# Ten of the 31 taps of three depthwise convolutions moved from VectorE to TensorE, in a two-layer hybrid decoder trunk

## What is computed

```python
a, gate = _split(h, (CONV_WIDTH, CONV_WIDTH))          # 512 channels each
z = a * jax.nn.sigmoid(gate)
z = jnp.pad(z, ((0, 0), (CONV_KERNEL - 1, 0), (0, 0)))   # CONV_KERNEL = 31
y = lax.conv_general_dilated(z, conv_w[:, None, :], ..., feature_group_count=CONV_WIDTH)
y = y + conv_b
return jax.nn.silu(_layernorm(y, ln_g, ln_b, LN_EPS))
```

## Time and profile before

| | us |
|---|---|
| median of 3 runs | 1245.67 (1244.42 to 1250.74) |
| profiled execution, its own time | 1247.64 |
| its span, first to last instruction | 1245.8 |
| PE busy in the span | 1208.2 (97%) |
| VectorE / ScalarE / GpSimd busy | 635.9 / 405.9 / 497.3 |
| mean granted TensorE clock | 0.986 |

### The profile page before, as it was taken

One profiled execution on the slowest core, in us unless ns is written; L12 is line 12 of the kernel. 1 busy time (PEld: TensorE's weight loads), 2 busy tenths in 40 slices (PEclk: granted clock), 3 DMA queues, 4 the chain that ended last, 5 costly groups with the idle time before them and its releaser, 6 DMA issues. The chain is left out here.

```text
span 1245.8 us, 19823 instructions
## 1 busy us (share of the span) xinstructions
PE 1208.2 (97%) x7876; PEld 965.5 (78%) x7876; DVE 635.9 (51%) x1032; ACT 405.9 (33%) x582; POOL 497.3 (40%) x368
## 2 busy tenths in 40 slices
PE   7999999999999999999999999989999999999996
PEld 5877778888888888886777767657888888888885
DVE  5524655442114544455988878976545210444333
ACT  5634423222112222227444535443322211222110
POOL 0541435554445555544121201113545444555441
PEclk9999999999999999999999989979999999999998
DMA  7212222232232223322111001102223222223211
GB/s 278 102 68 68 80 90 71 98 101 102 101 101 81 90 99 102 101 102 69 35 69 35 36 35 36 36 2 95 75 101 101 102 101 100 72 97 101 102 67 68
DMA packets 17776, 104.97 MB, mean 84 GB/s; under 512 B 1968, under 2 KB 2480, under 8 KB 6064
## 3 DMA queue, kind: packets, MB, share of 16 engines
q1 hardware_dynamic: 17280, 103.67, 24.0%
q10 hardware_dynamic: 432, 0.38, 0.1%
HBM read 101.94 MB, written 2.10 MB: 84 GB/s over the span
## 5 line engine op out<-in xcount | busy, mean ns | idle before, releaser
L582 POOL TENSOR_TENSOR w_lo<-w_raw,w_hi 128x512 fp32r<-128x512 f32 x360 | 491.6, 1396 | 715.4 <-ACT w_hi L675 266.5
L1015 PE MATMUL ps<-h_hi,w_hi 128*128 128x512 f32 x688 | 275.9, 401 | 0.1
L1015 PE MATMUL ps<-h_lo,w_hi 128*128 128x512 f32 x688 | 268.4, 390 | 0.0
L1015 PE MATMUL ps<-h_hi,w_lo 128*128 128x512 f32 x688 | 268.4, 390 | 0.0
L675 ACT ACTIVATE w_hi<-w_raw 128x2048 fp32r<-128x2048 f32 x50 | 95.6, 1912 | 194.7 <-PE ps L1015 143.4
L1015 PEld LDWEIGHTS ps<-h_hi,w_hi 128*128 128x128 f32 x688 | 129.3, 188 | 37.4 <-issue 10.9
L1015 PEld LDWEIGHTS ps<-h_hi,w_lo 128*128 128x128 f32 x688 | 129.3, 188 | 27.6
L1015 PE MATMUL ps<-f_hi,w_hi 128*128 128x512 f32 x384 | 149.4, 389 | 0.0
L1015 PE MATMUL ps<-f_lo,w_hi 128*128 128x512 f32 x384 | 149.4, 389 | 0.0
L1015 PE MATMUL ps<-f_hi,w_lo 128*128 128x512 f32 x384 | 149.4, 389 | 0.0
L1015 PEld LDWEIGHTS ps<-h_lo,w_hi 128*128 128x128 f32 x688 | 129.5, 188 | 25.7 <-issue 1.0
(11 more groups left out here) (328 smaller groups left out, 1705.1 us busy)
## 6 DMA issues: line engine op xcount, KB each, us to landing
w_raw<-in_weights SPq DMA_DIRECT2D x91, 1024.0 KB, 4.9
x<-in_xT SPq DMA_DIRECT2D x8, 256.0 KB, 6.3
w_raw<-in_weights SPq DMA_DIRECT2D x8, 256.0 KB, 6.9
outT<-x SPq DMA_DIRECT2D x8, 256.0 KB, 2.0
sgu_ln<-in_sgu_ln SPq DMA_DIRECT2D x1, 512.0 KB, 7.2
low_w<-in_low_w SPq DMA_DIRECT2D x1, 512.0 KB, 5.7
...
```

Of the source, the lines that this page charges most:

```text
L582: piece = pool.tensor_tensor(w_lo[:, j, at], w_raw[:, j, at], w_hi[:, j, at].bitcast(f32), SUB)
L1015: mm = pe.matmul(bank(gb(g) if isinstance(i, int) else g % 2), w, r, start=(k == 0 and m == 0), stop=(k == K - 1 and m == 2))
```

## The change

TensorE takes the last ten taps (j = 21 to 30) of groups 1, 2 and 3. ScalarE makes, for each of these 30 taps, a diagonal matrix: the 128x128 identity times the tap's weight of each partition (`diag`, into one of the two halves of a new buffer `tapd`). PE multiplies this diagonal by the shifted window of `zpad` (`ptap`, a float32 matmul of 128x128 by 128x512) and sums five taps in one PSUM tile, so there are two such tiles in each group. They have tile numbers of their own at the end of chunks 6, 8 and 10 of the projection, and so they use banks 0 and 1 in turn with the projection's tiles. VectorE adds each of the six sums to `cv` by one instruction (`padd`): those of groups 1 and 2 before tap 0, those of group 3 after taps 9 and 19. Group 0 keeps its 31 taps on VectorE. Several one-off semaphores are merged into one, `set_up`, with rising counts; the mask buffer is smaller by 896 bytes per partition. All three lists are written anew.

```diff
-MIX1 = [2] * 11
+MIX1 = [2, 2, 2, 2, 2, 2, 4, 2, 4, 2, 4]
+PE_CHUNK = {1: 6, 2: 8, 3: 10}
+PE_TAPS = 5
+PE_AFTER = {1: (0, 0), 2: (0, 0), 3: (10, 20)}
+N_V = [31, 21, 21, 21]
...
-        masks = sb("masks", [P, 4104], u8)
+        masks = sb("masks", [P, 3208], u8)
...
+            tapd = sb("tapd", [P, 2, P])
...
+        def pe_tile(c, q):
+
+            return FIRST_TILE[N_MIX1 + PE_CHUNK[c]] + 2 + q
+
+        def pe_tap(c, j):
+
+            return 2 * PE_TAPS * (c - 1) + j - N_V[c]
...
         PE1 = [
...
+            ("slice", 8, 4), ("slice", 8, 5), ("tok_tr", 1, 0), ("slice", 8, 6), ("slice", 8, 7),
+            *run("slice", 10, 0, 7), ("scores", 1, 1), ("slice", 10, 7), ("tok_tr", 1, 1), ("tok_tr", 1, 2),
+            ("scores", 1, 2), *run("ptap", 1, 21, 28), ("scores", 1, 3), ("ptap", 1, 28), ("ptap", 1, 29),
+            ("zw", 2), ("ptap", 1, 30), ("za", 2), ("tx", 1, 3, 0), ("tx", 1, 3, 1), ("post", 0, 0),
+            ("dx", 1, 3, 0), ("dx", 1, 3, 1), *run("slice", 9, 0, 8), ("tx", 1, 4, 0), ("tx", 1, 4, 1), ("ks", 2),
...
+            ("slice", 11, 0), ("dx", 1, 6, 0), ("dx", 1, 6, 1), *run("slice", 11, 1, 8), ("ptap", 2, 21),
+            ("g", 1, 0), ("ptap", 2, 22), ("ptap", 2, 23), ("u", 1, 0), ("s", 1, 0), ("ptap", 2, 24),
+            ("ptap", 2, 25), ("post", 0, 2), ("bonus", 2), ("g", 1, 1), ("corner", 2), ("ptap", 2, 26), ("y", 1, 0),
+            ("u", 1, 1), ("slice", 13, 0), ("slice", 13, 1), ("s", 1, 1), ("y", 1, 1), ("ptap", 2, 27),
+            ("ptap", 2, 28), ("g", 1, 2), ("ptap", 2, 29), ("ptap", 2, 30), ("u", 1, 2), ("s", 1, 2), ("y", 1, 2),
...
+            *run("slice", 21, 4, 8), ("tok_tr", 3, 0), ("scores", 3, 1), *run("ptap", 3, 21, 24), ("scores", 3, 2),
+            ("tok_tr", 3, 1), *run("ptap", 3, 24, 27), ("tok_tr", 3, 2), ("post", 2, 0), ("scores", 3, 3),
+            ("ptap", 3, 27), ("ptap", 3, 28), ("tx", 3, 3, 0), ("tx", 3, 3, 1), ("dx", 3, 3, 0), ("dx", 3, 3, 1),
+            ("tx", 3, 4, 0), ("tx", 3, 4, 1), ("post", 2, 1), ("dx", 3, 4, 0), ("dx", 3, 4, 1), ("ptap", 3, 29),
+            ("ptap", 3, 30), ("tx", 3, 5, 0), ("tx", 3, 5, 1), ("conv_mean", 0), ("dx", 3, 5, 0), ("dxt", 3, 5),
...
         ACT1 = [
...
+            ("evac_q", 8), ("diag", 1, 21), ("tok_tr", 1, 0), *run("diag", 1, 22, 29), ("cut", 54, 0),
+            ("cut", 54, 1), ("diag", 1, 29), ("cut", 54, 2), ("tok_tr", 1, 1), ("diag", 1, 30), ("zw", 2),
...
+            ("g", 3, 0), ("u", 3, 0), ("g", 3, 1), ("u", 3, 1), ("conv_sq", 0), ("conv_sq", 1),
+            ("cut", 58, 3), ("g", 3, 2), ("u", 3, 2), ("conv_sq", 2), ("conv_sq", 3), ("m", 1), ("m", 2),
...
+            def diag_(c, j):
+                i = pe_tap(c, j)
+                if i >= 2:
+                    group, n = divmod(i - 2, PE_TAPS)
+                    if n == PE_TAPS - 1:
+                        act.wait_ge(s("gemm_done"), pe_tile(1 + group // 2, group % 2) + 1)
+                    else:
+                        act.wait_ge(s("ptap_mm"), (PE_TAPS - 1) * group + n + 1)
+                act.activation(tapd[:, i % 2, :], IDENT, ACT.Copy, scale=col("conv_w", TAPS * c + j)).then_inc(s("tapd_done"), 1)
...
+            def ptap(c, j):
+                i = pe_tap(c, j)
+                q, n = divmod(j - N_V[c], PE_TAPS)
+                g = pe_tile(c, q)
+                pe.wait_ge(s("tapd_done"), i + 1)
+                if n == 0:
+                    pe.wait_ge(*freed(g))
+                    pe.wait_ge(*evacuated(g1(15 + 2 * c)))
+                    pe.wait_ge(*set_up("zpad"))
+                mm = pe.matmul(bank(g % 2), tapd[:, i % 2, :], zpad[:, c % 2, j:j + SEQ], start=(n == 0), stop=(n == PE_TAPS - 1))
+                mm.then_inc(s("gemm_done" if n == PE_TAPS - 1 else "ptap_mm"), 1)
...
             def tap(c, j):
...
-                if j == 0:
+                if j == 0 and not (c and PE_AFTER[c][0] == 0):
                     ts(cv[:, c, :], zpad[:, c % 2, 0:SEQ], col("conv_w", TAPS * c), col("conv_b", c), MUL, ADD)\
...
+            def padd(c, q):
+                g = pe_tile(c, q)
+                dve.wait_ge(s("gemm_done"), g + 1)
+                if PE_AFTER[c][q] == 0 and q == 0:
+                    ts(cv[:, c, :], bank(g % 2), col("conv_b", c), 0.0, ADD, ADD).then_inc(s(f"gemm_evac{g % 2}"), 1)
+                else:
+                    dve.wait_ge(*in_cv(c, PE_AFTER[c][q], q))
+                    tt(cv[:, c, :], cv[:, c, :], bank(g % 2), ADD).then_inc(s(f"gemm_evac{g % 2}"), 1)
```

More of the change, by code:

```diff
@@ L385, in build @@
         PE1 = [
[L386 to L405, removed]
@@ L488, in build @@
-            ("s", 3, 1), *run("tap", 3, 25, 31), ("s", 3, 2), ("m", 2), *run("conv_sub", 0, 4), ("conv_root",),
-            ("conv_scale", 0), ("conv_scale", 1), ("post_v", 3, 0), ("conv_scale", 2), ("conv_scale", 3),
-            ("post_v", 3, 1), ("m", 3), ("post_v", 3, 2), ("m", 4), ("post_v", 3, 3), *run("m", 5, 8),
+            ("zero", 0), ("zero", 1), ("stat",), *run("zero", 2, 6), ("evac_a", 0), ("evac_b", 0), ("evac_a", 2),
+            ("evac_b", 2), ("evac_a", 4), ("zero", 6), ("evac_b", 4), ("evac_a", 3), ("scan", 0), ("evac_b", 3),
@@ new lines, in build @@
+            ("dyn", 2, "rk"), ("evac_a", 11), ("s", 1, 0), ("bonus", 2), ("tap", 1, 16), ("post_v", 0, 3),
+            ("padd", 2, 0), ("evac_b", 11), ("corner", 2), ("s", 1, 1), ("solve", 2, 6), ("solve", 2, 5),
+            ("solve", 2, 4), ("solve", 2, 3), ("solve", 2, 2), ("padd", 2, 1), ("s", 1, 2), *run("tap", 2, 0, 6),
+            ("scores", 2, 0), *run("tap", 2, 6, 9), ("scores", 2, 1), ("scores", 2, 2), ("tap", 1, 17),
+            ("scores", 2, 3), ("solve", 2, 1), ("x_of", 2), ("scan", 3), ("tap", 2, 9), ("tap", 2, 10),
@@ new lines, in build @@
+            ("u", 1, 0), ("diag", 2, 24), ("diag", 2, 25), ("cut", 55, 3), ("diag", 2, 26), ("evac_q", 11),
+            ("diag", 2, 27), ("scores", 2, 0), ("g", 1, 1), ("u", 1, 1), *run("diag", 2, 28, 31), ("cut", 56, 0),
+            ("g", 1, 2), ("u", 1, 2), ("g", 1, 3), ("u", 1, 3), ("tok_tr", 2, 0), ("ysb", 1), ("tok_tr", 2, 1),
+            ("cut", 56, 1), ("tok_tr", 2, 2), ("cut", 56, 2), ("cut", 56, 3), ("zw", 3), ("za", 3), ("ksq", 3),
[5 rows of a table added]
+            ("cut", 57, 3), ("diag", 3, 21), ("diag", 3, 22), ("cut", 58, 0), ("diag", 3, 23), ("tok_tr", 3, 0),
@@ L525, in build @@
+            ("diag", 3, 24), ("diag", 3, 25), ("cut", 58, 1), ("diag", 3, 26), ("diag", 3, 27), ("tok_tr", 3, 1),
+            ("diag", 3, 28), ("post", 2, 0), ("tok_tr", 3, 2), ("tx", 3, 3, 0), ("tx", 3, 3, 1), ("diag", 3, 29),
[4 rows of a table added]
+            ("g", 3, 3), ("u", 3, 3), ("conv_root",), ("ysb", 3), ("post", 3, 0), ("conv_silu", 0), ("m", 3),
+            ("conv_silu", 1), ("conv_silu", 2), ("m", 4), ("m", 5), ("conv_silu", 3), ("m", 6), ("m", 7),
         ]
@@ L2107, in _ @@
                      "s": s_,
-                     "post_v": post, "tap": tap, "conv_sub": conv_sub, "conv_root": conv_root, "conv_scale": conv_scale, "m": m}
+                     "post_v": post, "tap": tap, "padd": padd, "conv_sub": conv_sub, "conv_root": conv_root, "conv_scale": conv_scale, "m": m}
             for name, *a in DVE1:
```

249 lines of the change are left out of this document (134 added, 115 removed), and 47 rows, old and new, of tables (ACT1, PE1).

## The result

The changed kernel took 1274.22 us (median of four runs, 1271.51 to 1277.15) against 1245.11 for the kernel before beside it: 1.0213 times as long, 95% interval 1.0190 to 1.0237. Forecast were 1259 us and a range of 1250 to 1270. The direction was right, and the loss, 24 to 30 us, is about twice the +13.4 of the sum. A later set of runs gave 1.0228 (1.0205 to 1.0252). The profiled execution took 1277.15 us, the longest of the four.

The account below looks back on a forecast made before the run. PE was taken as the bound in layer 1's mixing. The terms 28.6 + 1.0 - 1.8 - 2.4 - 7.2 - 4.0 - 0.8 = +13.4 us on 1245.7 gave 1259 us, range 1250 to 1270.

Parts of the forecast that it names:

- smaller mask buffer: Mask buffer shortened, grouped with merged semaphores and reordered early chunks: same instructions, no new kind of wait, so no cost.
- 30 taps: PE's 30 added float32 matmuls in layer 1's mixing, 0.955 us each, all on the path: +28.6 us.
- diagonals: ScalarE's 30 diagonals are covered work, but PE waits for a delayed `cut` at three or four places: +1.0 us.
- PE's idle time (`Sp`, 710 to 730): PE's 1.8 us wait for `Sp` in the tail ends; group 2's taps fill 2.6 us idle in chunk 1.
- clock (720 to 730 and tail): Taps filling PE's idle places keep the clock up: -4.6 us at 720 to 730, -4.0 in the tail.
- fewer switches: Places where slices begin among PE's other matmuls fall from 60 to 48, 0.2 us each: -2.4 us.
- `w_lo` behind the stage: An earlier `cut` 58 on ScalarE halves PE's 1.6 us wait for `w_lo` behind the stage: -0.8 us.
- All of PE's slack comes back: VectorE's relief lets the lists fill every idle place and the clock holds: +0.4 us, 1246 us; 7 in 100.
- VectorE sets the pace: VectorE's chain of taps ends layer 1's mixing stage, so its 18.7 us come off: 1227 us; 5 in 100.
- Diagonals pace the taps: Each tap's matmul on PE waits 0.38 us for its diagonal: +23.8 us, 1269 us; 10 in 100.
- Nothing comes back: New waits replace the old and the clock falls elsewhere: +27.2 us, 1273 us; 10 in 100.

Follow-up runs that it names:

- e1_masks_only: The kernel before with only the mask buffer made 896 bytes per partition smaller; 1259.35 us, 1.0107 of the kernel before.
- aligned change: The changed kernel with 128 more bytes behind the mask buffer, so operands moved by 768 bytes instead of 896; 1263.06 and 1262.35 us in two sets.
- r2_aligned_again: Second set of runs of the aligned change, beside the changed kernel as it is; 1262.35 us, 1.0121 of the kernel before.
- e3_lists_alone: The aligned change with its 30 TensorE taps put back on VectorE and no diagonals, all new lists kept; 1279.31 us, 1.0267 of the kernel before.
- e7_two_diagonals: The aligned change with only the first two diagonals made and reused by all later taps; 1264.37 us, 1.0147 of the kernel before.

## Why the forecast was wrong

| step | forecast | measured |
|---|---|---|
| smaller mask buffer | 0 | +13 (1.0228 against 1.0121), 11 at the same clock |
| 30 taps | +28.6 | +28.0 |
| diagonals | +1.0 | 0 |
| PE's idle time (`Sp`, 710 to 730) | -4.4 | -6.6 |
| clock (720 to 730 and tail) | -8.6 | -6.3, -0.7 and +2.8 in three profiles; -4 to -7 in the mean of ten executions |
| fewer switches | -2.4 | -2.4 to -3.1, as the rest |
| `w_lo` behind the stage | -0.8 | 0 to -1.5 |
| all but the mask buffer | +13.4 | +14 to +15 |

**The step that failed** is "The merged semaphores, the smaller mask buffer, `zero` before `stat` and the new order of the three early chunks cost nothing: same instructions". The instructions are the same, but their operands aren't in the same place: the matmuls of the MLP's second product became 3% slower each, on a PE that is full there, with no wait to show it. `e1_masks_only` makes the mask buffer smaller and nothing else, and gives 1.0107; the other items of the step were not tried one by one, but the sum without the mask buffer leaves no room for a cost of theirs above 1 or 2 us. With the step at its price the forecast for the median would have been 1259 + 13 = 1272 us.

**The rest of the sum held.** By the table under "The lists" the stage's growth can be added up for three profiled executions. For the aligned change in its second set (`r2_aligned_again`):

```profile
546.10:860.90 314.80, 306.02 (x3333) 218.76 (x3331) 229.03 (x469) 147.04 (x319) 63.91 (x48) 0.98 0.13 44
835.00:840.00 5.00, 3.92 (x79) 2.72 (x79) 2.46 (x6) 3.33 (x8) 4.22 (x4) 0.69 0.00 0
840.00:845.00 5.00, 4.62 (x132) 3.69 (x132) 2.64 (x4) 0.82 (x3) 0.73 (x1) 0.50 0.61 206
845.00:850.00 5.00, 5.00 (x55) 4.17 (x52) 1.88 (x3) 3.37 (x5) 0.00 (x0) 0.78 0.02 7
```

Here the clock was low for 10 us alone, which cost 4.6 us against 10.9 before. 28.0 of taps, less 6.6 of idle time, less 6.3 of clock is +15.1; the stage grew by 12.6, 2.5 less. For the change as it is, 28.0 - 6.7 - 0.7 is +20.6, and measured is +18.2, 2.4 less; for the first profile of the aligned change 28.0 - 6.7 + 2.8 is +24.1, measured +21.0, 3.1 less. What remains is about the 2.4 us forecast for fewer switches. `e3_lists_alone` points the same way: it has the matmuls of before in the new order, and PE's work is 4.7 us less.

**The clock term had the right sign, a part of its size, and the wrong places.** It took the low clock as the mark of two idle places, to be healed by filling them. Filled, the first did stay up, and the clock fell elsewhere, for less time in the mean: 22 us of an execution of the aligned change against 35 before, worth 4 to 7 of the 8.6 us forecast. One profile can't tell this. The clock was low in the stage for 10.2 us in one profile of the aligned change and for 27.3 in the other, with stages of 314.8 and 323.2 us; the latter profile, and that of the change, are of the longest execution of their set.

Idle time alone does not account for the falls. Ahead of those at 620 and 690 us PE is recorded busy for all of the 15 us before, with small matmuls at their end, as in the timeline above; ahead of the one at 765 for all but 0.3 us; only the last, at 855, comes after 15 us with 2.9 us of idle time. The Trainium skill, TensorE: Matmul & The Clock Gate, section HAM oscillation, ties such falls in real kernels to gaps in which PE is idle; the fall at 720 to 730 before fits that, and those at 620 and 690 after do not. As the ends of matmuls are modelled, what the array really did in these stretches can't be read more closely.

**The rivals.** "All of PE's slack comes back" and "VectorE sets the pace" are refuted: VectorE lost 12.1 us of work in the stage (242.1 to 230.0) and the stage grew. "Diagonals pace the taps" is refuted by `e7_two_diagonals` and by PE's weight loads, which waited 3.6 us in all for `tapd`, under the matmuls. "Nothing comes back" gave 1273 us, within 2 us of the result, and is wrong nonetheless: 13 of these microseconds came from another place, and idle time and clock did come back. VectorE's relief was also smaller than forecast, 12.1 us for 18.7; its taps are slower (0.796 for 0.757 us), which is 3.6 us on 92 of them. Why they are slower was not tried; it is not the addresses, as they take 0.796 in the aligned change too and 0.758 in `e1_masks_only`.

**What the experiments on the lists can and cannot price.** Without the taps on TensorE (`e3_lists_alone`), and with six of thirty, the new lists are slower than with them: what is saved in work turns into waits for VectorE and, as much or more, into low clock. So an experiment that takes taps out of the changed kernel makes them look free, and one that adds some shows their full price; only the comparison with the old lists gives what the change is worth.
